# Forty projection tiles computed as blocks of seven half-depth products

## The reference

```python
h = rms_norm(x, norm_g[layer])
proj = h @ w_in[layer]
u_ssm, z_ssm, q, k, v, z_attn, q_mem, z_mem, gate_logits = jnp.split(proj, split_at, axis=-1)
...                       # S5 state-space branch -> y, dilated attention -> o_attn, memory attention -> o_mem
o_ssm = y * jax.nn.silu(z_ssm)
o_attn = o_attn * jax.nn.silu(z_attn)
o_mem = o_mem * jax.nn.silu(z_mem)
gates = jax.nn.sigmoid((gate_logits + b_gate[layer]).astype(jnp.float32))
merged = (gates[:, :, 0] * (o_ssm @ w_br_ssm[layer]) + gates[:, :, 1] * (o_attn @ w_br_attn[layer])
          + gates[:, :, 2] * (o_mem @ w_br_mem[layer]))
x = x + merged @ w_out[layer]
return rms_norm(x, final_norm_g)
```

## Time and profile before

| | |
|---|---|
| median of three runs | 2456.36 us (2455.45 to 2456.59) |
| profiled execution | 2455.0 us from its first to its last instruction; the page gives no other time of it |
| granted TensorE clock, mean | 0.999 of full speed (2.4 GHz) |
| PE / PE weight loads | 2438.3 us (99%) / 1981.9 us (81%) busy |
| DVE / ACT / POOL | 1397.7 us (57%) / 588.0 us (24%) / 190.4 us (8%) busy |
| HBM | 245.10 MB read, 131.43 MB written |

### The profile page before, as it was taken

How to read it: one execution, slowest core, us unless ns; L and a number is a source line. 1 busy time by engine, 2 the same in 40 slices (tenths; PEclk the granted TensorE clock), 3 DMA queues, 4 the chain that set the end, 5 groups by cost and what they waited for, 6 DMA issues and landing times.

```text
span 2455.0 us, 31834 instructions
## 1 busy us (share of the span) xinstructions
PE 2438.3 (99%) x12622; PEld 1981.9 (81%) x12622; DVE 1397.7 (57%) x2636; ACT 588.0 (24%) x1275; POOL 190.4 (8%) x328
## 2 busy tenths in 40 slices
PE   9999999999999999999999999999999999999998
PEld 8888888888877777787777788888888888888887
DVE  7356776767734444413544443444345778787785
ACT  5222222222211111113333343333251111110201
POOL 0000000000011111110000000011100000000000
PEclk9999999999999999999999999999999999999999
DMA  8232433343454444442332343477654865857571
GB/s 327 99 93 76 106 114 117 107 120 95 115 151 137 149 160 142 151 156 73 105 134 95 121 147 122 161 228 243 205 206 164 285 182 168 248 177 242 159 233 59
DMA packets 171033, 378.67 MB, mean 154 GB/s; under 512 B 27008, under 2 KB 72164, under 8 KB 163717
## 3 DMA queue, kind: packets, MB, share of 16 engines
q1 hardware_dynamic: 134980, 235.03, 31.0%
q0 software_dynamic: 34864, 139.51, 16.9%
q10 hardware_dynamic: 1040, 2.10, 0.2%
HBM read 245.10 MB, written 131.43 MB: 153 GB/s over the span
## 4 chain that ended last, share of the span: by engine, by line
PE 97%; DVE 1%; ACT 1%; issue 0%; DMA 0%; DVEq 0%; SPq 0%; ACTq 0%
PE bank L137 29%; PE bank L139 29%; PE bank L138 28%; PE bank L2285 2%; PE bank L2328 1%; PE bank L2306 1%; PE bank L2194 1%; PE bank L2197 1%; PE bank L2264 1%; PE bank L2180 1%; PE bank L2242 1%; PE bank L2316 1%; ACT tsc L1188 1%; PE bank L2145 0%; PE bank L2247 0%
## 5 line engine op out<-in xcount | busy, mean ns | idle before, releaser
L137 PE MATMUL bank<-h_hi,w_hi 128*128 128x512 f32 (+1 forms) x2720 | 1083.7, 398 | 1.4 <-DVE h_lo L1434 1.4
L139 PE MATMUL bank<-h_hi,w_lo 128*128 128x512 f32 (+1 forms) x2720 | 1057.4, 389 | 0.0
L138 PE MATMUL bank<-h_lo,w_hi 128*128 128x512 f32 (+1 forms) x2720 | 1056.3, 388 | 0.0
L137 PEld LDWEIGHTS bank<-h_hi,w_hi 128*128 128x128 f32 x2720 | 510.8, 188 | 117.2 <-issue 13.6
L139 PEld LDWEIGHTS bank<-h_hi,w_lo 128*128 128x128 f32 x2720 | 510.7, 188 | 108.1
L138 PEld LDWEIGHTS bank<-h_lo,w_hi 128*128 128x128 f32 x2720 | 511.3, 188 | 103.0 <-issue 1.7
L129 DVE CAST w_hi<-w_raw 128x1024 fp32r<-128x1024 f32 (+1 forms) x121 | 83.3, 688 | 310.1 <-PE bank L139 294.3
L137 PE MATMUL bank<-h_hi 128*128 128x512 f32 (+1 forms) x464 | 172.5, 372 | 2.7 <-issue 1.5
L139 PE MATMUL bank<-h_hi,h_lo 128*128 128x512 f32 (+1 forms) x464 | 170.4, 367 | 0.0
L138 PE MATMUL bank<-h_lo,h_hi 128*128 128x512 f32 (+1 forms) x464 | 170.3, 367 | 0.0
L956 POOL DMA_DIRECT2D proj_d<-ev x160 | 88.9, 556 | 931.5 <-ACT ev L1148 560.1
(11 more groups left out here) (267 smaller groups left out, 2166.6 us busy)
## 6 DMA issues: line engine op xcount, KB each, us to landing
proj_d<-ev POOLq DMA_DIRECT2D x160, 256.0 KB, 2.9
w_raw<-w_in SPq DMA_DIRECT2D x68, 512.0 KB, 4.9
gt<-proj_d POOLq DMA_DIRECT2D x32, 768.0 KB, 7.6
proj_d<-ev POOLq DMA_DIRECT2D x22, 1024.0 KB, 4.9
w_raw<-w_br SPq DMA_DIRECT2D x32, 512.0 KB, 4.2
wx_raw<-w_br SPq DMA_DIRECT2D x32, 512.0 KB, 4.5
o_d<-ev POOLq DMA_DIRECT2D x12, 1024.0 KB, 6.9
ev<-o_d SPq DMA_DIRECT2D x12, 768.0 KB, 4.4
```

The costliest lines, as they stand in the source:

```text
L137: nc.tensor.matmul(out, ah, bh, start=(start and n == 0), stop=False)
L138: nc.tensor.matmul(out, ah, bl, start=False, stop=False)
L139: last = nc.tensor.matmul(out, al, bh, start=False, stop=(stop and n == len(pairs) - 1))
```

## The change

The 40 last tiles are taken in 20 pairs. For a pair of tiles (the two rows of a 2x2 matrix of weights), the two halves of the depth (its columns) and a pair of token chunks, the four output chunks were eight half-depth products. They are now seven, by the Strassen-Winograd scheme: the products are called A11, S2, S4, A12, S3, A22 and S1 after the weight factor that stands in each. A product is 4 depth slices, 12 matmuls. There are 40 such blocks (20 pairs of tiles by two pairs of chunks), and in place of 8 x 40 half-depth products of 12 matmuls there are 7 x 40.

What this takes beside it:

- Weight factors S1 to S4 are sums of weight quarters, made by POOL (`sum_s1` to `sum_s4`, four 128x512 operations a block). All seven factors are split in two: the high part by ACT (`factor_hi`), the low part by DVE (`factor_lo`, it stands in the same step as `factor_hi`, behind the step's slots), 128x512 each. Before, DVE did both halves of one 128x1024 tile.
- Token operands: three of the seven are h itself, four are sums of quarters of h. POOL makes them beside the tables (`make_operands`, eight rounds of eight 128x512 operations at tiles 6, 8 ... 20) and stores them in `hx_d`. Which chunks are paired changes twice (after blocks 7 and 27), and then all seven operands are loaded, split by ACT (`operand_hi`) and DVE (`operand_lo`, two 128x1024 subtractions each) and put in the place of the old ones, one after each product of the last block of a stage.
- Outputs: ACT copies the first product out (`keep_p1`); A12 adds onto it in its bank, S3 onto S2, S4 onto S1; DVE makes u2, u3, C21, C22 and C12 with five additions of a bank and a buffer (`add_u2` and so on); ACT then applies SiLU or tanh to C11 from PSUM and to the other three from SBUF (`finish_c11` and so on). Ten SBUF buffers hold what is in flight.
- A product step v is 12 matmuls. S4 of a block is multiplied two steps into the next block. Each product waits for the addition that frees its bank, two steps after the bank's last product.
- The slots of side work stay 8 to a block, but one comes after every 3.5 depth slices (10.5 matmuls) and not after every 4. `scan_pair` is cut in two: its second part, `turn_back`, stands one slot later on DVE.
- Weights are loaded in quarters (256 KB), all four of a pair again for each of its two blocks; `load_a21` stands at step 2 of the block before, and POOL's first sum that reads it at step 4.

The core of the diff:

```diff
+        NPR, NBK, NPAIRS = 7, NT - N_Z, (NT - N_Z) // 2
+        A11, S2, S4, A12, S3, A22, S1 = range(NPR)
+        SWAPS = (N_SILU - 1, N_SILU + NPAIRS - 1)
+        N_STEPS = NPR * NBK + 3
+        def step_of(b, i):
+            return NPR * b + (NPR + 2 if i == S4 else i)
+        def triples_before(j):
+            return 7 * (j + 1) // 2
...
+        def bank(b, group):
+            return psum[(b + {"c11": 0, "u": 1, "c21": 2, "c22": 0}[group]) % 3][:, :]
+        def product_bank(b, i):
+            return bank(b, ("c11", "u", "c22", "c11", "u", "c21", "c22")[i])
...
@@ POOL @@
+                def sum_s2(b):
+                    pool.wait_ge(*count(ws_done, SUM[S3, b]))
+                    pool.wait_ge(*count(wl_done, PREP[A11, b]))
+                    nc.gpsimd.tensor_tensor(w_a11, w_s1, w_a11, ALU.subtract).then_inc(ws_done[0], 1)
...
@@ ACT @@
+                for v in range(N_STEPS):
+                    row, at = divmod(v, NPR)
+                    if at == 0:
+                        factor_hi(row, A12)
+                        finish_c21(row - 1)
+                    if at == 1:
+                        keep_p1(row)
+                        finish_c22(row - 1)
+                        factor_hi(row, S3)
+                    if at == 2:
+                        factor_hi(row, S1)
+                    if at == 3:
+                        factor_hi(row + 1, A11)
+                    if at == 4:
+                        finish_c11(row)
+                        finish_c12(row - 1)
+                        factor_hi(row, S4)
+                    if at == 5:
+                        factor_hi(row + 1, A22)
+                    if at == 6:
+                        factor_hi(row + 1, S2)
+                    for swap in SWAPS:
+                        done = product_at(v - 5) if v >= 5 else None
+                        if done is not None and done[0] == swap:
+                            operand_hi(stage_of(swap) + 1, done[1])
+                    if product_at(v) is not None:
+                        for j in slots_in(v):
+                            side_slot(j)
...
@@ DVE @@
+                for v in range(N_STEPS):
+                    row, at = divmod(v, NPR)
+                    if at == 0:
+                        add_c22(row - 1)
+                    if at == 2:
+                        add_u2(row)
+                    if at == 3:
+                        add_c12(row - 1)
+                    if at == 5:
+                        add_u3(row)
+                    if at == 6:
+                        add_c21(row)
+                    if product_at(v) is not None:
+                        for j in slots_in(v):
+                            side_slot(j)
+...
...
@@ PE @@
+                for v in range(N_STEPS):
+                    if product_at(v) is None:
+                        continue
+                    b, i = product_at(v)
+                    bank_ready(b, i)
+                    pe.wait_ge(*count(wl_done, PREP[i, b]))
+                    order = operand_order(stage_of(b), i)
+                    if order is not None and b in (0, SWAPS[0] + 1, SWAPS[1] + 1):
+                        pe.wait_ge(*count(ob_lo, 2 * order + 2))
+                    a_hi, a_lo = factor(b, i)
+                    b_hi, b_lo = operand(h_hi, i), operand(h_lo, i)
+                    for k in range(4):
+                        mm = three_pass(product_bank(b, i), [((a_hi[:, k, :], a_lo[:, k, :]), (b_hi[:, k, :], b_lo[:, k, :]))],
+                                        start=(k == 0 and i not in (A12, S3, S4)), stop=(k == 3),
+                                        onto=(i in (A12, S3, S4)))
+                        if k == 3:
+                            mm.then_inc(mul_done[0], 1)
+                        for j in slots_in(v):
+                            if triples_before(j) == 4 * (MADE[v] - 1) + k + 1:
+                                side_slot(j)
```

More of the change, by code:

```diff
@@ new lines, in step_of, with product_at, products, numbered @@
+        def step_of(b, i):
+            return NPR * b + (NPR + 2 if i == S4 else i)
+        def product_at(v):
+            row, i = divmod(v, NPR)
+            b = row - 1 if i == S4 else row
+            return (b, i) if 0 <= b < NBK else None
+        def products(v):
+            return sum(product_at(x) is not None for x in range(v + 1))
+        MADE = [products(v) for v in range(N_STEPS)]
+        def numbered(table, before=()):
+            n = {x: k + 1 for k, x in enumerate(before)}
+            for v in range(N_STEPS + NPR):
+                row, at = divmod(v, NPR)
+                for what, later in table.get(at, ()):
+                    if 0 <= row + later < NBK:
+                        n[what, row + later] = len(n) + 1
+            return n
@@ new lines, in build_program, with operand_order, stage_of @@
+        N_PLACES = 5
+        place, taken = {}, [-5, -4, -3, -2, -1]
+        for what, b in PREP:
+            at = taken.index(min(taken))
+            place[what, b] = (at, taken[at])
+            taken[at] = step_of(b, what)
+        def operand_order(stage, i):
+            order = (A11, S2, A12, S3, A22, S1, S4).index(i)
+            return (None, 0, None, 1, 2, 3, None)[order] if stage == 0 else 4 + 7 * (stage - 1) + order
+        def stage_of(b):
+            return sum(b > swap for swap in SWAPS)
@@ L173, in unit, with slots_in @@
+        def triples_before(j):
+            return 7 * (j + 1) // 2
+        GLU_FREE = [max(MADE[step_of(b, i)] for i, b in place if place[i, b][0] in ((0, 1), (3, 4))[s])
+                    for s in range(2)]
+        def slots_in(v):
+            g = MADE[v] - 1
+            return [j for j in range(8 * NBK) if 4 * g < triples_before(j) <= 4 * (g + 1)]
         def unit(n, c):
@@ new lines, in _ @@
+                for n in range(2, N_Z):
+                    if value_tile(n - 2) is not None:
+                        store_tile(n - 2)
+                    if value_tile(n - 1) is None:
+                        if n == 2:
+                            store_tile(0)
+                        store_tile(n - 1)
+                    q, odd = divmod(n - 6, 2)
+                    if 0 <= q < 8 and odd == 0:
+                        make_operands(q)
+                sum_s1(0)
+                sum_s3(0)
@@ L1142, in keep_chunk @@
[L1142 to L1151 removed]
+                    if c == 0 and n >= 2:
+                        act.wait_ge(stored[s], 16 * (n // 2))
@@ new lines, in operand_hi, with keep_p1 @@
+                def operand_hi(stage, i):
+                    act.wait_ge(*count(ob_loaded[i], 16 * (stage if i in IN_PLACE else stage + 1)))
+                    for half in range(2):
+                        ks = slice(2 * half, 2 * half + 2)
+                        nc.scalar.activation(operand(h_hi, i)[:, ks, :], operand(lo_raw, i)[:, ks, :],
+                                             ACT.Copy).then_inc(ob_hi[0], 1)
+                def keep_p1(b):
+                    if not 0 <= b < NBK:
+                        return
+                    act.wait_ge(*count(mul_done, MADE[step_of(b, A11)]))
+                    if b:
+                        act.wait_ge(*count(add_done, ADD["u3", b - 1]))
+                    else:
+                        act.wait_ge(mm_done, unit(N_Z - 1, 1) + 1)
+                    nc.scalar.activation(p1, bank(b, "c11"), ACT.Copy).then_inc(p1_done[0], 1)
@@ L1683, in scan_pair, with turn_back @@
                                                      ALU.mult, ALU.add).then_inc(scanned, 1)
+                def turn_back(p):
+                    i, j = p % R, p % 2
+                    wide = (P, 2, NC)
+                    turn = [csb[:, i, a, :].unsqueeze(1).to_broadcast(wide) for a in range(2)]
                     dve.wait_ge(scanned, 6 * p + 4)
```

607 lines of the change are left out of this document (483 added, 124 removed).

## The result

The changed kernel takes 2484.1 us (median of four runs, 2479.36 to 2487.01) against 2455.9 for the kernel before beside it: ratio 1.0113, 95% interval 1.0099 to 1.0127. Forecast were 2386 us; 2428 was the upper end of the range. The profiled execution took 2479.4 us, its span is 2477.6.

A forecast was written before the change was run, and what follows sets the result against it. PE, busy 99% of the span, was taken as the bound: 2455.0 - 109.1 + 20 + 16 + 1 + 1 + 1 = 2384.9, with the median 1.4 us above the span: 2386. Range for 8 in 10: 2352 to 2428.

The forecast's parts named there:

- the last S4: End of the stage: the final S4 product follows S1 at once and waits for C22, 1 us, once.
- I take the near end and no cost: POOL's weight sums in each block: taken at 0.685 us each, their chain to PE hidden within six steps, no cost.
- 1 us on it in all: Operand sums beside the tables: eight rounds of eight, 5.5 us against 7.4 us of DVE slack, 1 us in all.
- the forecast of 1680: DVE's busy time in the whole kernel: 286 us more, to some 1680.
- a spare of 6.3: DVE in a scan block: 19.8 us of work while PE takes 26.1 us, leaving 6.3 us spare.
- The rival of GpSimd as the bound: Weight sums in each block: each holds DVE up for its whole length, harmless to 1.8 us; 2546 at 2.8; chance 0.06.
- Attention's turn: PE's turn in attention: 1.1 us of wait at each of 20 turns, taken as 20 us, bounds 4 and 40.
- Swaps: Operand exchanges after blocks 7 and 27: DVE's extra subtractions cost 8 and 8 us, bounds 6 and 30 together.
- The first operands: DMA loads of the first operands: 1 us.
- Late factors: Rival on weight factors in the stage: PE waits 1 us a block for S2 or S3, 40 us more, 2426; chance 0.19.

The follow-up runs named there:

- the kernel without the four costs: Changed kernel with weight and operand sums on GpSimd mostly cut to 8 of 512 columns, bank additions behind side slots, no operand swaps: 2393.8 us.
- the paced kernel with the early load: Changed kernel with weight sums on DVE, additions behind slots, odd turns later, operand sums one per unit, last a21 load a step earlier: 2475.3 us.

## Why the prediction was wrong

**Right.** 480 matmuls fewer, 109.1 us; the unchanged pace behind the stage; which waits would come: turns, operands at the swaps, the last S4 (2.0 us for 1). No wait of PE on POOL itself.

**The step that failed** is "I take the near end and no cost" for POOL's sums, with its companion "1 us on it in all" for the tables. I had the chain S1 to S2 on GpSimd and found it hidden; the cost wasn't in that chain. It was in DVE, which lost 0.57 us for each sum in the stage and 1.08 us beside the tables, 150 us of its time; without them its 1820 us would be 1670, near the forecast of 1680. Removing them gave 28 and 19 us. The sentence on the Trainium skill had the mechanism and the length right, and then said that 5.4 us a block lie inside a spare of 6.3. Measured are 2.3 us a block, less than half of that, and they cost 28 us all the same. That was the error of reasoning: the spare is an average over a block, and PE waits at deadlines. An operation lengthened just ahead of one is paid in full while DVE idles later. The rival of GpSimd as the bound used the same average, and so put the harmless limit at 1.8 us a sum; harm came at 1.4.

**Mis-sized.** Attention's turn: 20 us forecast; the ledger has 37.5 of excess in the waits for tsc (35.5 in the view above), and 14.0 more at the low clock. Half of these waits are DVE's order, additions ahead of the batch: with the additions behind the slots they halved. The contention isn't their cause, for with the weight sums small or on DVE they stayed. What the other half comes from wasn't run. My count took one addition for each hit turn; in the step shown there are two additions and two lengthened subtractions. Swaps: 16 forecast, 21.6 measured, inside its bounds. The first operands: 1 forecast; in the kernel without the four costs PE still loses 7 us in four waits between 681 and 698 us.

**Not in the sum.** The clock: some 27 us. I read 1.00 in all stretches before and never asked what PE's new idle time would do to it. And the last a21 quarter. SP issued it behind the large loads that follow attention; SP, then POOL:

```profile
1796.86 1.23 SPq L1012 DMA_DIRECT2D w_raw<-w_in  x1
```

```profile
1807.27 1.26 POOL L1207 TENSOR_TENSOR keep<-w_raw 128x512 f32<-128x512 f32 x1 [18.11 <-DMA w_raw<-w_in]
```

It landed 10 us after its issue, and PE waited 8.8 us for the factor. Late factors had a chance of 0.19 as a loss of 1 us a block; it came to 20.8 us of waits in eight places, not all along.

**The balance.** The sum was 2384.9. With the four costs gone (37 us of them were in it) the kernel still has a span of 2394.7, not 2348; the 47 us between are what remains in the ledger's third column, 48.5 us above before. So of the 98 us between 2386 and the measured 2484.1 the sums that failed are some 46 (28 and 19, 1 forecast), the swaps 6, and about as much again as the sums is spread over waits for which no experiment has the cause. Which of these would go with a faster DVE alone, and what the wait for em (5.8 us in the ledger) comes from, was not tried.

## What to carry to other kernels

A helper engine with room is not a free engine: ask which ports it shares, and count what each of its operations adds to the busy engine. Set a new delay against the next deadline, not against the average spare of a block. When PE was at 99% with the clock full, price each new wait at its length and add what PE runs at the lower clock behind it. And of two remedies for a wait, see first whether both spend the same lead; of a paced transfer, look at what it now leaves beside.

## What the runs showed of the hardware

- GpSimd's sum of two 128x512 f32 tiles in SBUF: 1.32 to 1.46 us in the mean, DVE's 0.69. A DVE operation with all inputs in SBUF that starts behind it ends 0.55 us after it (0.68 became 1.49 us); a sum that starts behind the DVE operation ends 1.13 us or more after that (1.48 us); one with an input in PSUM isn't touched (686 ns throughout). DVE's 160 sums cost it as much when GpSimd made them: 1820.4 us busy against 1821.6.
- A DVE operation started while POOL is issuing a store ahead of its sum was held to the end of the sum in 22 of 24 cases (0.68 became 2.26 us).
- PE waited 29 times for 1.6 us or more between 60 and 1850 us of the changed kernel's trace; behind 16 of these waits (1.7 to 8.8 us) the granted clock fell to its lower level, behind 13 (1.6 to 3.0 us) it didn't. After PE had been idle for 2.0 us ahead of L138 at 1835.22 it fell, and matmuls of 128x512 started 0.43 us apart, not 0.227:

```profile
1835.22 0.50 PE L138 MATMUL bank<-h_hi,w_hi 128*128 128x512 f32 x1 [2.00 <-DVE ev L2319]
...
1836.32 0.63 PE L138 MATMUL bank<-h_hi,w_hi 128*128 128x512 f32 x1
1836.75 0.63 PE L139 MATMUL bank<-h_lo,w_hi 128*128 128x512 f32 x1
```

- A 128 KB store landed in 2.4 us alone, in 4.3 us beside one of another queue's stores of 1 or 1.8 MB, and in 7.4 us beside two (medians in the trace of the paced kernel with the early load).
